# A new beginning for a two-block transformer kernel: one small product for the bias lines, one root per token half, and constants loaded later

## The reference

```
u = _rms_norm(h, g_pre[i])            # y = x * rsqrt(mean(x*x) + 1e-6), then * g
cols = u @ w_in[i]                    # queries, keys, values; r, k, v, z, codes; gates
...
cols = cols + (prev - cols) * mu      # prev: the row of the token before (zeros for the first)
w_log = -softplus(-(w0 + tanh(wd) @ w_up)) - 0.5
a = sigmoid(a0 + ad @ a_up)
...
l_own = einsum('bhqd,bhjd->bhqj', qc, ko) + bias_h[:, _t5_bucket(dist_o)]
l_own = where(dist_o >= 0, l_own, -inf)
```

## Time and profile before

| | |
|---|---|
| median of three executions | 1959.03 us |
| the profiled execution | 1955.08 us |
| its span, first to last instruction | 1953.2 us |
| PE busy | 1882.9 us (96%) |
| DVE busy | 420.0 us (22%) |
| ACT busy | 288.9 us (15%) |
| mean granted PE clock | 0.988 |
| bytes moved | 485.28 MB, mean 248 GB/s |

### The profile page before, as it was taken

One profiled execution on the slowest core, in us unless ns is written; L12 is line 12 of the kernel. 1 busy time (PEld: TensorE's weight loads), 2 busy tenths in 40 slices (PEclk: granted clock), 3 DMA queues, 4 the chain that ended last, 5 costly groups with the idle time before them and its releaser, 6 DMA issues. The chain is left out here.

```text
span 1953.2 us, 28892 instructions
## 1 busy us (share of the span) xinstructions
PE 1882.9 (96%) x12954; PEld 931.8 (48%) x12954; DVE 420.0 (22%) x837; ACT 288.9 (15%) x570; POOL 83.8 (4%) x123
## 2 busy tenths in 40 slices
PE   7999999999999999999799999999999999999996
PEld 4476654456644454566444344443434434344442
DVE  3633333215410000245311010111101011010121
ACT  1210230223210000233111010100101011010110
POOL 0100000005000000051000000000000000000000
PEclk9999999999999999999799999999999999999998
DMA  9732217334144253443389999999999999999990
GB/s 281 252 130 88 77 71 259 109 136 172 44 143 159 91 189 102 175 154 136 110 293 384 354 390 365 371 379 358 383 374 366 381 358 386 351 390 378 368 403 28
DMA packets 220511, 485.28 MB, mean 248 GB/s; under 512 B 14365, under 2 KB 26269, under 8 KB 220254
## 3 DMA queue, kind: packets, MB, share of 16 engines
q1 hardware_dynamic: 212320, 471.49, 66.0%
q10 hardware_dynamic: 6702, 7.03, 1.2%
q0 software_dynamic: 1360, 4.85, 0.6%
HBM read 475.22 MB, written 8.14 MB: 247 GB/s over the span
## 5 line engine op out<-in xcount | busy, mean ns | idle before, releaser
L1284 PE MATMUL bank<-ring,work 128*128 128x512 f32 (+4 forms) x1632 | 673.9, 572 | 18.6 <-ACT work L1498 3.6
L1284 PEld LDWEIGHTS bank<-ring,work 128*128 128x128 f32 x1632 | 306.4, 192 | 357.5 <-issue 324.2
L2780 PE MATMUL bank<-ring,work 128*64 128x512 f32 x1792 | 396.9, 595 | 0.7 <-DVE work L2922 0.7
L2780 PEld LDWEIGHTS bank<-ring,work 128*64 128x64 f32 x1792 | 123.7, 137 | 239.5 <-issue 238.7
L2788 PE MATMUL bank<-ring,work 128*32 128x256 f32 x3584 | 205.0, 380 | 0.0
L2826 PE MATMUL bank<-ring,work 128*64 128x512 f32 x896 | 204.6, 598 | 0.0
L2788 PEld LDWEIGHTS bank<-ring,work 128*32 128x32 f32 x3584 | 110.7, 110 | 112.7 <-issue 45.4
L2951 DVE TENSOR_TENSOR work<-work,bank 64x512 f32<-64x512 f32 x56 | 38.7, 692 | 374.8 <-ACT work L2870 374.8
L2826 PEld LDWEIGHTS bank<-ring,work 128*64 128x64 f32 x896 | 59.3, 136 | 117.1 <-issue 117.1
L2835 PE MATMUL bank<-ring,work 128*32 128x256 f32 x1792 | 108.3, 382 | 0.0
L2835 PEld LDWEIGHTS bank<-ring,work 128*32 128x32 f32 x1792 | 52.5, 109 | 74.3 <-issue 45.4
(11 more groups left out here) (363 smaller groups left out, 1179.4 us busy)
## 6 DMA issues: line engine op xcount, KB each, us to landing
ring<-in_moe_w_gate SPq DMA_DIRECT2D x56, 2048.0 KB, 10.9
ring<-in_moe_w_up SPq DMA_DIRECT2D x56, 2048.0 KB, 9.4
ring<-in_moe_w_down SPq DMA_DIRECT2D x56, 2048.0 KB, 13.3
ring<-in_w_in SPq DMA_DIRECT2D x20, 2048.0 KB, 8.3
ring<-in_w_out SPq DMA_DIRECT2D x6, 2048.0 KB, 8.6
ring<-in_dense_w_gate SPq DMA_DIRECT2D x5, 2048.0 KB, 7.8
ring<-in_dense_w_up SPq DMA_DIRECT2D x5, 2048.0 KB, 7.9
ring<-in_dense_w_down SPq DMA_DIRECT2D x5, 2048.0 KB, 7.8
```

The source lines that it names most:

```text
L1284: mm = pe.matmul(banks(j)[:, 0:width], x[:, k0 + kt, tt * P:(tt + 1) * P], w[:, kt, c0:c0 + width], start=first and n == 0, stop=last and ...
L2780: mm = pe.matmul(out[half, :], xgT[:, k, 0:64], w[n][:, k, :], start=(k == 0), stop=(k == KD - 1))
```

## The change

`begin` loses its phase: its instructions are issued into the same block as those of `first_mixers`, with banks from the common rotation, and nothing meets at its end.

- **Bias lines.** The table itself, 33 by 8, is the stationary operand of a single product, so the bank holds one line per head on 8 partitions (`line_rows`). ACT copies it once. One transfer of 2 MB writes each line 128 times (`unsqueeze(1).broadcast_to`). It stands behind all of ACT's small loads, ahead of the tanh. DVE's wait for the written lines is gone, ACT's ahead of the askew read stays.
- **Root.** Each token half has its own semaphore for its arrival, its own square root (with the epsilon as bias of the activation) and its own reciprocal.
- **Zeros.** The zero row is written from 128 partitions by 17 numbers.
- **Loads.** Positions and frequencies go to ACT's queue. SP issues the factors for `codes` (64 KB) ahead of the weights of `k`, the other factors (1 MB) between `k` and `r`. The eleven constants of later stages are issued by SP when the first block's `yb` is done.

```
@@ first_mixers
+                if name == "codes":
+                    pe.wait_ge(*core.x_turned[tt])
...
+        act.wait_ge(*core.line_left)
+        act.dma_start(core.lines[:, 0:P * BANK].rearrange("h (p n) -> h p n", n=BANK),
+                      core.line_rows[0:AH, :].unsqueeze(1).broadcast_to([AH, P, BANK])).then_inc(core.lines_written, 16)
...
-        dve.wait_ge(core.mu_in, 16)
-        dve.wait_ge(core.zeros_written, 16)
+        dve.wait_ge(core.mu_in[0], 16)
         split("codes", 0)
         split("codes", 1)
+        dve.wait_ge(core.mu_in[1], 16)
...
-        dve.wait_ge(core.lines_written, 32)
@@ begin
+        core.load_weights(sp, 0, most=1)
+        sp.dma_start(core.mu[:, codes:RW], spread(a["mu_shift"][0, codes:RW], P)).then_inc(core.mu_in[0], 16)
+        core.load_weights(sp, 0, most=2)
+        sp.dma_start(core.mu[:, 0:codes], spread(a["mu_shift"][0, 0:codes], P)).then_inc(core.mu_in[1], 16)
+        core.load_weights(sp, 0, most=3)
...
+        pe.wait_ge(table_in, 16)
+        pe.wait_ge(marking_in, 16)
+        banks.fill(pe.matmul(banks(line)[0:AH, :], table[0:REL_BUCKETS + 1, :], marking[0:REL_BUCKETS + 1, :],
+                             start=True, stop=True))
...
+        for tt in range(NT):
+            dve.wait_ge(core.rows_in[tt], 16)
+            dve.tensor_tensor_reduce(scaled[:, tt, :], h[:, tt, :], h[:, tt, :], 1.0 / DM, 0.0, ALU.mult, ALU.add,
+                                     stat[:, 0, tt:tt + 1]).then_inc(sum_ready, 1)
+        for tt in range(NT):
+            dve.wait_ge(root_ready, tt + 1)
+            step(dve.reciprocal(stat[:, 2, tt:tt + 1], stat[:, 1, tt:tt + 1]))
+            dve.tensor_scalar(scaled[:, tt, :], h[:, tt, :], stat[:, 2, tt:tt + 1], None, ALU.mult).then_inc(rows_scaled, 1)
...
+        act.wait_ge(zero_row, 2)
+        act.dma_start(core.shift_rows[0, :].rearrange("(p n) -> p n", p=P), nothing).then_inc(core.zeros_written, 16)
+        for tt in range(NT):
+            act.wait_ge(sum_ready, tt + 1)
+            nc.scalar.activation(stat[:, 1, tt:tt + 1], stat[:, 0, tt:tt + 1], ACT.Sqrt, bias=core.eps).then_inc(root_ready, 1)
+        act.wait_ge(*banks.ready(line))
+        banks.leave(nc.scalar.copy(core.line_rows[0:AH, :], banks(line)[0:AH, :]), line)
@@ program, behind sp.wait_ge(core.yb_done, NT)
+                sp.dma_start(core.router, a["moe_router_2"][0].rearrange("(k p) e -> p k e", p=P)).then_inc(core.later_in, 16)
+                for key, view in gains.items():
+                    if key != "g_pre":
+                        sp.dma_start(view, sources[key].rearrange("(k p) -> p k", p=P)).then_inc(core.later_in, 16)
+            load_squares(core, sp, core.later_in, "before", "ones", to=dict(before=core.before, ones=core.ones))
```

More of the change, by code:

```diff
@@ L1074, in begin @@
     stat = core.main.take(3, NT)
-    nothing = core.main.take(RW)
+    nothing = core.main.take(RW // P)
+    assert core.main.at <= core.mu_at
     core.shift_rows = nc.dram_tensor("shift_rows", (SEQ + 1, RW), F32, kind="Internal").ap()
-    core.lines = line = nc.dram_tensor("bias_lines", (AH, P * BANK + BANK), F32, kind="Internal").ap()
-    blocks = [(tt, k0) for tt in range(NT) for k0 in (0, 4)]
+    core.lines = nc.dram_tensor("bias_lines", (AH, P * BANK + BANK), F32, kind="Internal").ap()
@@ L1079, in begin @@
     gain = gains["g_pre"]
[L1080 to L1167, removed]
@@ new lines, in begin, with _ @@
+    table_in, marking_in, last_row, zero_row, sum_ready, root_ready, rows_scaled = (core.new_semaphore(n) for n in (
+        "table_in", "marking_in", "last_row", "zero_row", "sum_ready", "root_ready", "rows_scaled"))
+    line = banks.new("scalar")
+    blocks = [(tt, k0, banks.new("vector")) for tt in range(NT) for k0 in (0, 4)]
+    core.x_turned = [banks.left(blocks[2 * tt + 1][2]) for tt in range(NT)]
+    codes = IN_COLS["codes"][0] - 4 * AW
+    @core.block.sync
+    def _(sp):
+        for tt in range(NT):
+            sp.dma_start(h[:, tt, :], a["x"][0, tt * P:(tt + 1) * P, :]).then_inc(core.rows_in[tt], 16)
+        load_squares(core, sp, core.ident_in, "ident", to=dict(ident=core.ident))
+        with nc.allow_non_contiguous_dma("gains, one feature per partition"):
+            sp.dma_start(gain, sources["g_pre"].rearrange("(k p) -> p k", p=P)).then_inc(core.ident_in, 16)
+        core.load_weights(sp, 0, most=1)
[3 more added lines that the diff above has]
+        core.load_weights(sp, 0, most=3)
@@ new lines, in _ @@
+    @core.block.gpsimd
+    def _(pool):
+        pool.memset(table, 1.0).then_inc(last_row, 1)
+        pool.memset(core.eps, EPS).then_inc(zero_row, 1)
+        pool.memset(nothing, 0.0).then_inc(zero_row, 1)
+    @core.block.tensor
+    def _(pe):
+        pe.wait_ge(table_in, 16)
+        pe.wait_ge(marking_in, 16)
+        banks.fill(pe.matmul(banks(line)[0:AH, :], table[0:REL_BUCKETS + 1, :], marking[0:REL_BUCKETS + 1, :],
+                             start=True, stop=True))
+        pe.wait_ge(core.ident_in, 32)
+        for tt, k0, j in blocks:
+            pe.wait_ge(rows_scaled, tt + 1)
+            for k in range(k0, k0 + 4):
+                mm = pe.transpose(banks(j)[:, (k - k0) * P:(k - k0 + 1) * P], scaled[:, tt, k * P:(k + 1) * P], core.ident)
+            banks.fill(mm)
@@ L1168, in begin @@
+    core.line_left = banks.left(line)
     core.main.back(mark)
@@ L3254, in program @@
         low_at = main.at
-        core.mu = main.whole[:, low_at + NT * (AW + BW + 2 * DM) - RW:low_at + NT * (AW + BW + 2 * DM)]
-        main.take(NT, AW + BW + 2 * DM)
-        begin(core, a, bias_rows, gains, sources)
-        main.back(low_at)
+        core.mu_at = low_at + NT * (AW + BW + 2 * DM) - RW
+        core.mu = main.whole[:, core.mu_at:core.mu_at + RW]
+        core.banks = Banks(core)
+        begin(core, a, gains, sources)
         ya, yb = main.take(NT, AW), main.take(NT, BW)
@@ L3298, in _ @@
             sp.wait_ge(core.yb_done, NT)
+            with nc.allow_non_contiguous_dma("gains, one feature per partition; eight logits' weights per row"):
+                sp.dma_start(core.router, a["moe_router_2"][0].rearrange("(k p) e -> p k e", p=P)).then_inc(core.later_in, 16)
[3 more added lines that the diff above has]
+            load_squares(core, sp, core.later_in, "before", "ones", to=dict(before=core.before, ones=core.ones))
             sp.dma_start(core.causal, causal_dram).then_inc(core.later_in, 16)
```

36 lines of the change are left out of this document (25 added, 11 removed).

## The result

The changed kernel took 1974.86 us (median of 4 runs, 1973.20 to 1977.74), the kernel before 1958.34 beside it (median of 4, 1955.39 to 1963.87). The ratio is 1.0083, 95% interval 1.0057 to 1.0108: slower by 0.8%, where I had forecast 1948. The profiled execution went from a span of 1953.2 to 1971.4 us, 18.2 more.

A forecast was written before the change was run, and what follows sets the result against it. PE, busy 1882.9 of 1953.2 us, was taken as the bound, so an earlier start moves the rest. -14.8 + 3.0 + 0.8 = -11.0 us gave 1944.1 against the profiled 1955.08, 1948 for a median; range 1944 to 1952, 8 in 10 within 1943 to 1967.

The forecast's parts named there:

- third term: Line write beside the third round trip and the factors behind it: 0.8 us lost, bounds 0 and 3.
- Rival 1: Line write is slow and holds the queues, say 40 us: 1960 to 1967, centre 1963; chance 0.26.
- first term: Beginning, up to `k`'s product: it starts at 17.5 instead of 32.3, 14.8 us gained, bounds 12 and 17.
- my own test: At the start: the step on the start is wrong if `k`'s product begins after 20 us.
- second term: Round trip of `codes` before the code transposes: now late for PE, 3 us lost, bounds 0 and 6.
- The rest costs nothing: Dropped copies and waits, and eleven moved loads near 310 us: no extra cost, 30 us of cover stay.
- The third round trip: Shifted columns in the first block: POOL's third addition some 11 us earlier than 79.33.
- The tests that I named for a wrong sum: Line write lands after 60 us, or `v`'s weights or `k`'s write take twice as long from issue to landing.
- the sum: Whole kernel: -14.8 + 3.0 + 0.8 = -11.0 us, giving 1944.1 for the profiled execution and 1948 for a median.

The follow-up runs named there:

- e1: Changed kernel with the line write from 128 partitions (16 copies per head, each written 8 times): 1950.82 us, ratio 0.9973 to the kernel before.
- e3: Changed kernel with the line write from partitions 0 to 15, two copies of each head, 64 repeats: 1964.08 us, ratio 1.0036 to the kernel before.
- e10: Changed kernel, line write left on partitions 0 to 7, with both changes of SP's order as in e5: 1971.98 us, ratio 1.0059 to the kernel before.
- e5: e1 with `k`'s weights issued before the codes' mu, and each shifted product's write before the load of weights after next: 1941.97 us.
- e2: Changed kernel with the eight source lines on partitions 0, 4, ... 28, each head's column copied four times: 1949.86 us, ratio 0.9957 to the kernel before.
- e7: e1 with only `k`'s weights issued ahead of the codes' mu: 1950.24 us, ratio 0.9959 to the kernel before.
- e9: e8 with ACT's parameter loads waiting until `k`'s weights have landed and the tanh moved ahead of the small matrices: 1941.25 us.
- e6: e1 with only each shifted product's write issued ahead of the load of the weights after next: 1946.63 us, ratio 0.9933 to the kernel before.
- b1: Kernel before with only the eleven late constants moved behind the first block: 1957.52 us, ratio 0.9994.
- e8: e5 with the line write issued behind the second half's factor copies, its read behind the first silu: 1941.31 us, ratio 0.9917 to the kernel before.
- e4: Changed kernel, write still from partitions 0 to 7, issued behind the second half's factor copies and read behind the first silu: 1949.19 us, ratio 0.9961.

## Why the prediction was wrong

**The step that failed is the third term**, the write of the lines. I had bounds of 12 and 93 us and took the side near the row, 12 to 20; it took some 46. The row I leaned on, 6.4 us for 1 MB, was a write from 128 partitions. The new one differed in partitions, repeats and shape, and e1 to e3 show that the partitions decide. The term was 0.8 us. With the source alone changed (e1) the kernel is 24.0 us faster by the medians, 11 parts in a thousand or some 21 us by the ratios; under the better order (e10 against e5) it is 30 us.

The Trainium skill was nearer than I was. "SBUF — State Buffer", the section on the port swizzle, has four neighbouring partitions share a port at 27.6 GB/s; for two ports that is the estimate of 55 GB/s and 38 us which stood in the prediction. Here it was 49 GB/s from partitions 0 to 7 (45 from the issue to the last packet), 100 from 0 to 15 (e3) and 205 at a step of four (e2), so the rule of fours holds and the estimate of 55 was a tenth to a fifth too high. What the section of "DMA: Bandwidth & Descriptors" on the semaphore's 16 makes of an outer dimension of eight, eight engines, agrees too: from 50 to 54 us the write took 45.9% of the 16 engines, 7.3 of them, and e3's 16 rows took 94.4%, 15.1. A rule of a page against the change, with no row to contradict it, deserved more than 0.26.

**Rival 1 is what happened**, by its mechanism: a write of 40 us, priced at 0.31 us a packet (measured 0.30), that gives every other packet to the weights (128 to 128). Its price, 1960 to 1967, was too low by 8 to 15 us for three reasons. I let two weight loads be late by 10 us each; `v`'s took 40 where before it took 9.8. It stands in SP's queue behind the read of the codes, which landed only at 60.8; from 60 to 76 us SP's queue sent 352 packets and the line write 352. That its share on the eight slow engines waited for that read is my reading of these rows. I had the codes themselves through before the write hurt, and their read alone took 18 us more. And "worse with a cold PE clock" had no number: the second half of `r`, 16 passes, took 9.31 us where it was 7.03. How the 8 to 15 us divide among the three isn't measured.

**The first term was 11.7, not 14.8**, just outside its bounds, and by my own test (`k` after 20) it was wrong. Six kernels whose queues begin alike gave 10.8 to 13.7 (`k` at 21.49 in e2, 18.61 in e1), so a part of the miss is spread from run to run. Up to the end of `codes` it was pessimistic: `codes` began at 12.37 (said 12.2) and took 3.7 us, not 5.3, at the fast spacing. The weights of `k` were late. Their issue at 7.41 stood behind 3.79 us that SP spent on issuing the codes' mu; with that order changed `k` began at 17.73 (e10), but e7 gained only 0.4 us on e1 by it. And ACT's loads shared the engines, as e9 shows (16.62 without them, for 18.74). The term also left out that `k` would start behind an idle time, at a granted clock of 0.50: 3.1 us more in the changed kernel, 2.0 in e5. But the term's size hardly matters: e9 gained 2 us there and lost them again.

**The second term** said 3 us, bounds 0 to 6. With the write cured (e1) it is 5.0; the codes' write was issued at 20.18 (said 19.6) and landed at 37.69 (said 33.5 to 38). The range given for the landing doesn't follow from its own figures: 9.2 + 2.2 - 2.5 = 8.9 MB at 0.32 to 0.27 MB/us from 10 us on end at 38 to 43. PE was free to go at 44.44, not by 43, and came 1.6 us later than said, so that the term is within its bounds in part by luck. And e5 and e6 show that it need not be there: by the order of issues it is 0.

**The rest costs nothing**: right (b1). **The third round trip**, said to be 11 us earlier, came 20 us later (99.05 for 79.33). The tests that I named for a wrong sum, a line write that lands after 60 us, or `v`'s weights or the write of `k` twice as long as before (40.0 for 9.8 and 36.8 for 10.3), are all met.

The kernel that the sum described, with the order as it is and a write that isn't in the way, is e1: 1950.82 for 1948, in the range given. That e5's span, 1941.7 against 1953.2, is -11.5 and the sum was -11.0 is luck. In e5 the terms are 13.4 gained by the start, 2.0 lost by `k`'s slow passes, and nothing lost at the codes and the factors. In medians e5 is 16 us ahead of before: its profiled execution was 1.5 us above its median, that of before 3 us below. The start of before varies as well. In b1, profiled at its median, the second eight passes of the line products took 7.19 us for 4.14, and `codes` began at 30.08 for 26.46. Only one execution of before was profiled, so whether its median runs look like that isn't shown.

## What to carry to other kernels

Price a DMA out of the partitions by where they lie: here 0 to 7 gave 49 GB/s and 0 to 15 gave 100, where eight at a step of four gave 205. The slow transfer occupied its DMA engines all the while, so it was the others that paid, more the longer it lasted (13.3 us for 25.7, 24.0 us for 46). Spread the source (every fourth partition, or copies made by a product that is there anyway) or issue it where nothing else is under way. When a beginning is made earlier, look again at each queue's order, since a transfer that had been covered by the old beginning (here the codes' write, behind 2 MB of weights) can be uncovered with it.

## What the runs showed of the hardware

- A write with each row repeated 64 or 128 times: 2 MB in some 46 us from partitions 0 to 7, 25.7 us from 0 to 15, and at most 18 us from eight partitions at a step of four (e2). From all 128 partitions, 8 repeats a row, 11.8 and 16.6 us beside other transfers (e1, e5) and 7.2 us late (e8).
- The sharing is not always one packet for one. From 64 to 70 us of the changed kernel it was (128 to 128); from 44 to 50 us SP's queue sent 425 packets for the write's 144, and the write took less than half of the engines' time (45.8%); in e3 from 40 to 50 us SP's queue moved nothing although the read of the codes was issued at 39.85. Why is open.
- Some of SP's issues are long: beside the line write 4.44 and 9.48 us for one load and one write at 39.82 and 44.30, where the same two take 0.47 and 0.58 in e4. It isn't the slow write alone: the codes' write took 4.81 us to issue at 23.11, ahead of it, and 6.30 in e1. Why is open.
- The start of `k` lay between 18.61 and 21.49 us in the six kernels that issue the codes' mu first (e1, e3, e6, the changed one, e4, e2), and between 17.73 and 18.94 in the four that issue `k`'s weights first (e10, e7, e8, e5). One execution of each was profiled, and no run isolates the spread.
